# Who copies the logits out of PSUM in the stick-breaking attention stage: VectorE before, ScalarE after

## The reference, cut to what matters

```python
z = jnp.einsum('bhqd,bhkd->bhqk', qb, kf) * scale
causal = key_pos[None, :] < q_pos[:, None]
log_beta = jax.nn.log_sigmoid(z)
log_keep = jnp.where(causal, log_beta - z, 0.0)
between = lax.cumsum(log_keep, axis=3, reverse=True) - log_keep
w = jnp.where(causal, jnp.exp(log_beta + between), 0.0)
return jnp.einsum('bhqk,bhkd->bhqd', w, vf)
```

## Time and profile before

| | |
|---|---|
| time, median of 3 runs | 3494.41 us (3491.72 to 3497.82) |
| the profiled execution: its own time | 3497.59 us |
| its span, first to last instruction | 3495.8 us |
| TensorE busy | 3112.3 us, 89% |
| VectorE busy | 1773.6 us, 51% |
| ScalarE busy | 1186.1 us, 34% |
| GpSimd busy | 1089.1 us, 31% |
| the attention stage | from about 92 us to about 475 us |

### The profile page before, as it was taken

One profiled execution on the slowest core, in us unless ns is written; L12 is line 12 of the kernel. 1 busy time (PEld: TensorE's weight loads), 2 busy tenths in 40 slices (PEclk: granted clock), 3 DMA queues, 4 the chain that ended last, 5 costly groups with the idle time before them and its releaser, 6 DMA issues.

```text
span 3495.8 us, 36734 instructions
## 1 busy us (share of the span) xinstructions
PE 3112.3 (89%) x14488; PEld 2568.4 (73%) x14488; DVE 1773.6 (51%) x1804; ACT 1186.1 (34%) x1880; POOL 1089.1 (31%) x426
## 2 busy tenths in 40 slices
PE   5888789999989999999887898899976689999997
PEld 4666568887878888888676677688855567777786
DVE  5788843112253444444666334577744746656533
ACT  2666720001131000000322223577742425555511
POOL 2111024444424444444345232111122022121152
PEclk9999999999999999999887898999997889999998
DMA  2000021112211111111112111200031110000131
GB/s 94 19 25 31 19 90 48 49 49 68 71 31 49 49 49 49 49 49 49 43 49 102 37 67 52 79 31 25 31 126 37 55 36 25 31 25 31 55 115 67
DMA packets 44572, 178.99 MB, mean 51 GB/s; under 512 B 4672, under 2 KB 5696, under 8 KB 43392
## 3 DMA queue, kind: packets, MB, share of 16 engines
q1 hardware_dynamic: 32976, 119.89, 10.8%
q10 hardware_dynamic: 11440, 56.89, 4.2%
HBM read 147.40 MB, written 29.36 MB: 51 GB/s over the span
## 4 chain that ended last, share of the span: by engine, by line
PE 71%; DVE 10%; issue 10%; ACT 5%; POOL 2%; DMA 1%; SPq 0%; ACTq 0%; DVEq 0%; POOLq 0%
PE ps L456 47%; PE ps L1022 4%; PE aux L933 3%; PE ps L872 2%; PE ps L917 2%; PE ps L576 1%; PE ob L500 1%; PE ps L478 1%; PE ob L952 1%; PE ob L955 1%; PE ob L953 1%; POOL wh L413 1%; PE aux L935 1%; DVE zb L1789 1%; PE aux L605 1%
## 5 line engine op out<-in xcount | busy, mean ns | idle before, releaser
L413 POOL TENSOR_TENSOR wh<-raw,con 128x1024 fp32r<-128x1024 f32 x211 | 512.8, 2430 | 2345.5 <-PE ps L456 1209.4
L415 POOL TENSOR_TENSOR wl<-raw,wh 128x1024 fp32r<-128x1024 f32 x211 | 576.2, 2731 | 16.5
L456 PE MATMUL ps<-hh,wh 128*128 128x512 f32 x1536 | 480.2, 394 | 29.1 <-POOL wl L415 11.4
L456 PE MATMUL ps<-hl,wh 128*128 128x512 f32 x1536 | 477.8, 392 | 0.0
L456 PE MATMUL ps<-hh,wl 128*128 128x512 f32 x1536 | 476.6, 392 | 0.0
L456 PEld LDWEIGHTS ps<-hh,wh 128*128 128x128 f32 x1536 | 290.4, 190 | 92.2 <-issue 18.4
L456 PEld LDWEIGHTS ps<-hl,wh 128*128 128x128 f32 x1536 | 291.4, 190 | 61.5
L456 PEld LDWEIGHTS ps<-hh,wl 128*128 128x128 f32 x1536 | 291.1, 190 | 61.3
L1669 DVE TENSOR_TENSOR px_l<-px,px_h 128x512 fp32r<-128x512 f32 (+3 forms) x288 | 214.1, 745 | 115.6 <-ACT px_h L1526 113.4
L1911 DVE TENSOR_TENSOR y_t<-y_t,ps 128x1024 f32<-128x1024 f32 x120 | 146.5, 1221 | 174.5 <-PE ps L456 174.5
L1259 ACT ACTIVATE ff<-fr 128x1024 f32<-128x1024 f32 x32 | 33.9, 1061 | 552.9 <-DVE fr L1900 552.9
(11 more groups left out here) (353 smaller groups left out, 6299.2 us busy)
## 6 DMA issues: line engine op xcount, KB each, us to landing
raw<-wall SPq DMA_DIRECT2D x211, 512.0 KB, 3.5
spill_x<-x_t ACTq DMA_DIRECT2D x2, 4096.0 KB, 12.7
spill_out<-ot ACTq DMA_DIRECT2D x16, 512.0 KB, 2.6
go<-spill_out ACTq DMA_DIRECT2D x16, 512.0 KB, 5.9
xold_t<-spill_x ACTq DMA_DIRECT2D x2, 4096.0 KB, 16.4
x_t<-xt SPq DMA_DIRECT2D x8, 512.0 KB, 8.7
spill_o<-op ACTq DMA_DIRECT2D x4, 1024.0 KB, 3.8
o_all<-spill_o ACTq DMA_DIRECT2D x2, 2048.0 KB, 11.5
```

The lines of the kernel that those rows point to most:

```text
L413: pool.tensor_tensor(wh[:, s, :, :], raw[:, s, :, :], ones.unsqueeze(1).broadcast_to([P, KT, P]), ALU.mult).then_inc(w_high, 1)
L415: pool.tensor_tensor(wl[:, s, :, :], raw[:, s, :, :], wh[:, s, :, :].bitcast(F32), ALU.subtract).then_inc(w_split, 1)
L456: m = pe.matmul(ps[:, w, a:b], lw[:, sl, k, :], r[:, i, a:b], start=(i == 0 and j == 0), stop=(i == len(ks) - 1 and j == 2))
```

## The change

ScalarE gets the copy of the logits, between its exponential of unit b and its exponential of unit a. VectorE's copy goes. The two semaphores move along: the copy still increments `z_free`, and it still waits for `av_done` of the unit whose `zb` buffer it overwrites. VectorE's L1801 still waits for `z_free`.

```diff
@@ -1172,6 +1172,10 @@
                 act.wait_ge(d_ready, b + 1)
                 act.activation(zb_n, zb_n, ACT.Exp).then_inc(pw_ready, 1)
             if a < NU:
+
+                if a >= 3:
+                    act.wait_ge(av_done, a - 2)
+                copy(zb[a % 3][:, :, 0:n], zsrc[:, :, 0:n]).then_inc(z_free, 1)
                 act.wait_ge(abs_ready, a + 1)
                 act.activation(e, e, ACT.Exp, scale=-1.0).then_inc(ea_ready, 1)
             if 0 <= m < NU:
@@ -1806,14 +1810,6 @@
                     mask = con[:, C_MASK01 + 256 - c1:C_MASK01 + 256].unsqueeze(1).broadcast_to([P, 2, c1])
                     i = dve.tensor_tensor(e[:, :, 0:c1], e[:, :, 0:c1], mask, ALU.mult)
                 i.then_inc(sp_ready, 1)
-            if a < NU:
-                n = SB_UNITS[a][4]
-                dve.wait_ge(abs_ready, a + 1)
-
-                if a >= 3:
-                    dve.wait_ge(av_done, a - 2)
-                zsrc = ps[:, Z_SLOT, :].rearrange("p (h q) -> p h q", h=2)
-                dve.tensor_copy(zb[a % 3][:, :, 0:n], zsrc[:, :, 0:n]).then_inc(z_free, 1)
             if 0 <= m < NU:
                 n = SB_UNITS[m][4]
                 dve.wait_ge(sph_ready, m + 1)
```

## The result

| | before | change |
|---|---|---|
| time, median | 3494.41 us | 3512.83 us (5 runs, 3510.91 to 3522.47) |
| ratio to before | | 1.0056, 95% interval 1.0043 to 1.0068 |
| span of the profiled execution | 3495.8 us | 3509.3 us |
| first instruction of the next stage on VectorE | 473.75 us | 492.96 us |

The prediction was 3511.7, + 17.3; measured is + 18.4, and the interval of the ratio reaches from about + 15 to + 24. The stage itself ends 19.2 later in the profiled execution, whose span grew by 13.5 only: what follows the stage, the same instructions in both, happened to be 5.7 shorter there. Over all the profiles of this document that remainder lies between 3016.3 and 3024.1 us, whatever was done to the stage.

The account below looks back on a forecast made before the run. The prediction took a loop of dependences through ScalarE's queue as the bound, with no engine full. Paid copies of 10.6 in the first three pairs and 6.7 in the last gave 3494.4 + 17.3 = 3511.7 us, range 3502 to 3521.

Parts of the forecast that it names:

- The bound: Attention stage: no engine is full; a loop of dependences through three back-to-back ScalarE instructions, 6.76 us per unmasked last-pair step.
- The removal at nothing: VectorE, all steps: dropping 48 copies of 1.22 us at full width only lengthens its wait for `sp_h`; worth nothing.
- the earlier logits at nothing: TensorE: the copy releases the next logits sooner, but the triangle still waits 0.30 us for `sp_l`; worth nothing.
- The copy's price: ScalarE's queue ahead of exp(-|z|): 0.90 us per copy at width 1024, 0.7 at 768, 0.5 at 512; 35.2 in all.
- Which are covered: By the copied unit's position in its pair: paid where ScalarE's queue ends the step; 17.3 of 35.2 us paid.
- positions 3 and 11: First three pairs: slack between `sp_l` and triangle 0.76 and 0.26 us, so 0.14 and 0.64 of the copy paid.
- Position 9: First three pairs: VectorE is held up by GpSimd, so the copy costs 0; `sp_l` arrives 0.1 us before `wh` ends.
- the sign of being wrong: Unmasked steps staying at 6.8 us, or a position 9 step growing by more than half a microsecond.
- rival 5: Last pair: more pauses may lower TensorE's clock, + 2.5, 3514.2 us; within the 0.77 for slower by 10 to 26.
- The port cliff: Position 9, first three pairs: `sp_l` comes after GpSimd's `wl` began and waits; 1.8 us, 3513.5; within the shared 0.77.
- The `av_done` wait at nothing: ScalarE ahead of its copy: waiting for the weighted sum costs nothing, at most 0.1 us a step, 5 in all.
- The faster rival: Last pair and narrow masked steps: earlier logits and a relieved VectorE save some 8 us, 3486; chance 0.05.

Follow-up runs that it names:

- the second pass: The change plus ScalarE reading |z| out of PSUM once more between its copy and exp(-|z|), against the change: 3551.14 us, ratio 1.0165.
- one dose: The change itself, ScalarE making the copy once per unit and VectorE none, against the kernel before: 3512.83 us, ratio 1.0056.

## Why the prediction was right, point by point

- **The bound.** "A loop of dependences" through ScalarE's queue: shown from both sides. Nothing removed from VectorE mattered, every pass added on ScalarE did, and with that queue put in another order its steps got 0.25 to 0.8 shorter and the kernel faster.
- **The removal at nothing, and the earlier logits at nothing:** right, 0.9997.
- **The copy's price, 0.90 at full width:** the queue shows 0.90 exactly. The two full-price kinds of step, `k_h` and the outputs, grew by 0.90 and 0.69.
- **Which are covered.** About half of the 35.2 added was hidden, and the other side of it is ScalarE's waits for the logits ahead of |z|: 40.6 us over the stage before, 23.6 in the change. Positions 1, 7 and 10 cost nothing, positions 5 and 9 at most 0.12 for the copy itself. Position 4 was 0.14 for 0.2, position 0 0.49 for 0.5.
- **Two terms mis-sized: positions 3 and 11**, 0.31 and 0.79 for 0.14 and 0.64. The slack between `sp_l` and the triangle is not all slack. Where the triangle follows the logits without a pause, a full-width matmul takes 0.23 from start to start; after a wait the first takes 0.34 (460.43 to 460.77 above) and starts some 0.05 after its release. These 0.16 belong to the price once the wait is there: 0.90 - 0.26 + 0.16 = 0.80, and 0.90 - 0.76 + 0.16 = 0.30. Six steps, 1.0 in all.
- **Position 9, "Priced at 0, with a margin of only 0.1":** this price was wrong. The copy was covered, but the step grew by 0.9 twice, which is the sign of being wrong that the prediction names (more than half a microsecond). I looked for it at GpSimd's port; it was rival 5, the clock, in a stretch where I had not placed it. I had put that rival in the last pair only. Position 5, priced at 0 too, grew by 0.61 in pair 1, with the lower level on the first matmuls of the step. The port cliff is real, and the second pass fell off it in pair 1; one dose did not. The Trainium skill, "SBUF — State Buffer", says under "SBUF: two separate sides" that whichever of the two starts first has the port pair for its whole instruction. The traces of both kernels agree: `wl` lasts 3.26 when `sp_l` is first, and `sp_l` 3.30 when `wl` is.
- **The `av_done` wait at nothing:** right with TensorE at full clock. In one step of the last pair, at the low clock, ScalarE stood 0.51 for the weighted sum ahead of its copy:

```profile
440.27 1.02 ACT L1088 ACTIVATE zb<-ps 128x1024 f32<-128x1024 f32 x1 [0.51 <-PE ob L629]
```

- **The faster rival:** out. VectorE was busy for 81% of the stage, and still the kernel without its copy took 0.9997 of the time before.
- **The total is partly luck.** Against the 12.2 of the profile, the terms that were too small are 1.0 for positions 3 and 11, 1.9 for position 9 and 0.6 for position 5 of pair 1; position 2 of pair 2 gave 1.2 back, where a slow-clock step before was not one after. In the last pair, positions 3, 7 and 8 were 0.7 to 0.9 too small each and position 4 was 0.95 too large. At position 8 the miss is the clock's: 8.51 at a granted clock of 0.71, 7.65 at 1.00 with the pauses filled, where 7.69 was foreseen. Positions 3 and 7 had 0.60 and 0.76 where they had 1.00 before, but no experiment separates the clock there. So the mechanism and the prices of the copy were right, the term for the clock was put at nothing in the sum, and 17.3 came close to 18.4 also because such misses cancel.

## What to carry to other kernels

Before moving an instruction to the emptier engine, follow one period of the pipeline from releaser to releaser and ask in which gap of that engine it would land: ScalarE had 126 us to spare here, 80 of it ahead of the exponential of `zb` and 41 ahead of |z|, and the copy was put behind both. Where |z| waits for TensorE's logits anyway, the copy cost little or nothing; elsewhere it was paid. Price a moved instruction step by step, where each of the cases has its own slack, and count slack from where the waiting instruction could truly follow. Two cheap kernels tell a move apart into its halves: one with the work taken from the first engine and given to nobody, one with equal work added to the second.

## What the runs showed of the hardware that was not expected

- The granted clock decided steps in which the added instruction itself was free. With TensorE idle for 2.06 in place of 1.34 before position 9, the matmuls behind it went from 0.23 to 0.43 apart for part of the step and cost 0.9 us, in pairs 1 and 2 of both profiles; six matmuls on zeros in the pause brought it back. In pair 0 the same pause cost nothing.
- Around 100 us the same program ran at a granted clock of 1.00 or 0.72, and 4 us hung on that.
- An instruction with two SBUF inputs on VectorE that was issued 0.20 after GpSimd's had begun took 3.30 in place of 1.23; issued 0.66 before GpSimd's previous instruction ended, it got in ahead of the next.
